# Up projections with the tokens stationary, hidden values transposed and taken by the down projection chunk by chunk, stage boundaries by token tile

## The reference

```
# model 1, layer i
f = swiglu_ffn(rmsnorm(x, ffn1_norm_pre), w_in, w_out)    # 1024 -> 2 x 2816 -> 1024
x = x + 0.5 * rmsnorm(f, ffn1_norm_post)
x = x + rmsnorm(mixer(rmsnorm(x, mix_norm_pre)), mix_norm_post)
f = swiglu_ffn(rmsnorm(x, ffn2_norm_pre), ...); x = x + 0.5 * rmsnorm(f, ffn2_norm_post)
# swiglu_ffn: (silu(gate) * up) @ w_out
# model 2, layer i (ALPHA = 8 ** 0.25)
x = layer_norm(ALPHA * x + mixer(x))
x = layer_norm(ALPHA * x + square(relu(x @ w1)) @ w2)     # 1024 -> 4096 -> 1024
x = x + sigmoid(x @ w_gate) * (p @ w_proj)
```

## Time and profile before

| | |
|---|---|
| time, median of 3 runs | 3379.53 us (3378.67 to 3382.61) |
| span of the profiled execution | 3380.1 us |
| PE busy (union of matmuls) | 3065.2 us, 91% |
| DVE busy | 2050.7 us, 61% |
| ACT busy | 1397.9 us, 41% |
| weights read | 466 MB, 138 GB/s over the span |
| mean granted TensorE clock | 0.925 of full speed |

### The profile page before, as it was taken

One profiled execution on the slowest core, in us unless ns is written; L12 is line 12 of the kernel. 1 busy time (PEld: TensorE's weight loads), 2 busy tenths in 40 slices (PEclk: granted clock), 3 DMA queues, 4 the chain that ended last, 5 costly groups with the idle time before them and its releaser, 6 DMA issues.

```text
span 3380.1 us, 48537 instructions
## 1 busy us (share of the span) xinstructions
PE 3065.2 (91%) x18678; PEld 2694.5 (80%) x18678; DVE 2050.7 (61%) x3081; ACT 1397.9 (41%) x2230; POOL 74.2 (2%) x98
## 2 busy tenths in 40 slices
PE   8999888899999998888998889976999999987998
PEld 8989766789898986677997568864897989774897
DVE  5559887555555798856555455552656665553555
ACT  4446422343433552333434334442444345442444
POOL 0000000000000000000000000000000000000000
PEclk9999999899999999988998779986999999886999
DMA  6555211255455441114553235540554555421453
GB/s 215 186 163 170 86 50 51 99 166 187 164 181 175 163 156 38 57 49 158 186 187 119 71 109 187 181 141 6 184 187 163 175 182 184 162 94 50 153 187 137
DMA packets 127386, 469.89 MB, mean 139 GB/s; under 512 B 14318, under 2 KB 14494, under 8 KB 125904
## 3 DMA queue, kind: packets, MB, share of 16 engines
q1 hardware_dynamic: 124128, 452.62, 40.0%
q0 software_dynamic: 3056, 14.39, 1.2%
HBM read 465.91 MB, written 1.05 MB: 138 GB/s over the span
## 4 chain that ended last, share of the span: by engine, by line
PE 82%; DVE 10%; ACT 4%; issue 2%; POOL 1%; DMA 0%; SPq 0%; DVEq 0%; ACTq 0%
PE ps L469 81%; DVE hc L1623 1%; DVE w_lo_part L1422 1%; ACT w_hi_part L1034 1%; PE ps L537 1%; ACT gdn_w L1248 1%; POOL stats L2044 1%; DVE x_res L1546 1%; ACT h_hi_part L1050 0%; DVE x_res L1558 0%; DVE xn L1552 0%; DVE x_res L1525 0%; DVE h_lo_part L1438 0%; DVE lke L1865 0%; DMA w_raw<-in_weights 0%
## 5 line engine op out<-in xcount | busy, mean ns | idle before, releaser
L1422 DVE TENSOR_TENSOR w_lo_part<-w_raw,w_hi_part 128x1024 fp32r<-128x1024 f32 x856 | 1028.8, 1218 | 684.7 <-ACT w_hi_part L1034 684.2
L1034 ACT ACTIVATE w_hi_part<-w_raw 128x1024 fp32r<-128x1024 f32 x856 | 884.4, 1055 | 621.2 <-PE ps L469 615.5
L469 PE MATMUL ps<-h_hi_part,w_hi_part 128*128 128x256 f32 x3424 | 987.1, 288 | 16.5 <-DVE h_lo_part L1440 11.6
L469 PE MATMUL ps<-h_lo_part,w_hi_part 128*128 128x256 f32 x3424 | 983.3, 287 | 0.0
L469 PE MATMUL ps<-h_hi_part,w_lo_part 128*128 128x256 f32 x3424 | 982.7, 287 | 0.0
L469 PEld LDWEIGHTS ps<-h_hi_part,w_hi_part 128*128 128x128 f32 x3424 | 673.3, 197 | 24.3 <-issue 17.4
L469 PEld LDWEIGHTS ps<-h_lo_part,w_hi_part 128*128 128x128 f32 x3424 | 672.9, 197 | 0.6
L469 PEld LDWEIGHTS ps<-h_hi_part,w_lo_part 128*128 128x128 f32 x3424 | 672.2, 196 | 0.0
L469 PE MATMUL ps<-w_hi_part,h_hi_part 128*128 128x512 f32 (+2 forms) x812 | 329.8, 406 | 12.3 <-DVE h_lo_part L1438 7.0
L469 PE MATMUL ps<-w_hi_part,hid_lo_part 128*128 128x512 f32 x864 | 340.9, 395 | 0.0
L469 PE MATMUL ps<-w_lo_part,hid_hi_part 128*128 128x512 f32 x864 | 340.9, 395 | 0.0
(11 more groups left out here) (307 smaller groups left out, 2590.2 us busy)
## 6 DMA issues: line engine op xcount, KB each, us to landing
w_raw<-in_weights SPq DMA_DIRECT2D x856, 512.0 KB, 3.4
row<-in_rows POOLq DMA_DIRECT2D x8, 1024.0 KB, 4.9
row<-in_rows POOLq DMA_DIRECT2D x8, 512.0 KB, 4.4
const<-in_const SPq DMA_DIRECT2D x1, 1152.0 KB, 13.8
x_res<-in_x SPq DMA_DIRECT2D x1, 1024.0 KB, 5.3
ple_p<-in_p POOLq DMA_DIRECT2D x4, 256.0 KB, 4.9
out<-x_res SPq DMA_DIRECT2D x2, 512.0 KB, 2.6
cols<-in_cols SPq DMA_DIRECT2D x1, 422.0 KB, 7.1
```

What stands on the lines that cost most here:

```text
L469: return nc.tensor.matmul(out, lhsT, rhs_, start=start, stop=stop, skip_group_check=True)
L1034: A(w_hi[:, s, 0:wd], w_raw[:, s, 0:wd], ACT.Copy).then_inc(*up("w_hi", u))
L1422: V.tensor_tensor(w_lo[:, s, 0:wd], w_raw[:, s, 0:wd], w_hi[:, s, 0:wd].bitcast(F32), ALU.subtract).then_inc(*up("w_lo", u))
```

## The change

- Up projections: a unit of a new kind "G" holds two blocks of 128 inputs by 512 outputs (256 gate and 256 up columns in a gated FFN, 512 columns in an MLP). The tokens (h_hi, h_lo, 128 x 128) are stationary and 512 weight columns move: 12 matmuls of 512 columns a unit, four units a chunk, 11 chunks in a gated FFN and 8 in an MLP. The result has the tokens on the partitions.
- The hidden values of a chunk (256 or 512 features) are transposed on PE (turn_hidden: 4 or 8 transposes) after the second unit of the next chunk, taken to hid_hi by ACT and hid_lo by DVE, and used by the down projection right behind that chunk. The last chunk's are transposed inside the first down unit of the chunk before.
- The gated FFNs no longer normalise x before the up projection: x is turned raw, with the gain applied on the way out of PSUM, and the row's root is applied in silu's scale and in the gating.
- Stage boundaries: last_units runs by tile and by half (t, n) and signals each half. Updates of x are in halves of 512. Tile 0 of x is turned at the end of the old stage, ahead of the last three matmuls for an FFN; each tile and half is taken by take_tile; the first chunk of an FFN or MLP and the first four units of a ple gate run on tile 0 first and turn tile 1 before their fourth unit. The owed splits stand one by one between these steps.
- The first transfer of x is split in two and weight unit 0 goes between.

The diff, cut to its core:

```diff
+        for c in range(FF1_N + 1):
+            if c < FF1_N:
+                hidden(a, i, c * 256, FF1 + c * 256)
+            if c:
+                for k in range(2):
+                    rows(b, i, (c - 1) * 2 + k)
...
 PE
-            def last_units(tag, parts):
+            def last_units(tag, bank, parts, nxt):
+                for t, n in ((t, n) for t in range(NT) for n in range(2)):
+                    end = t == NT - 1 and n == 1
+                    for j, (hi, lo, ready) in enumerate(parts):
...
+                        if end and j == LAST - 1 and nxt and nxt.startswith("ffn"):
+                            begin_tile(nxt, 0)
...
+                if nxt and not nxt.startswith("ffn"):
+                    begin_tile(nxt, 0)
...
+                def up_unit(s, c, j, t):
+                    tok = slice(t * P, (t + 1) * P)
+                    out = ps[:, 2 * (c % 2) + t, :]
+                    for k in (2 * j, 2 * j + 1):
+                        w = slice((k % 2) * BANK, (k % 2 + 1) * BANK)
+                        mm(out, h_hi[:, k, tok], w_hi[:, s, w], k == 0, False)
+                        mm(out, h_hi[:, k, tok], w_lo[:, s, w], False, False)
+                        last_ = mm(out, h_lo[:, k, tok], w_hi[:, s, w], False, k == KC - 1)
...
+                def turn_hidden(c):
+                    pe.wait_ge(*when("hid_gated" if blocks == 2 else "hid_square", (tag, c)))
...
+                def down_unit(c, blk):
+                    pe.wait_ge(*when("hid_lo", (tag, c, blk // 2)))
...
+                        if t == 0 and c == n - 2 and blk == 0:
+                            turn_hidden(n - 1)
...
+                tail = [(c, blk) for c in (n - 2, n - 1) for blk in range(blocks)]
+                for c, blk in tail[:-LAST]:
+                    down_unit(c, blk)
...
 ACT, ffn
+                for c in range(n):
+                    weights(2)
+                    if c:
+                        take_hidden(c - 1)
+                    weights(2)
+                    act.wait_ge(*when("w_used", ("up", tag, c)))
+                    if gated:
+                        for t in range(NT):
+                            A(act_out[:, s, t, 0:256], ps[:, 2 * s + t, 0:256], ACT.Silu, scale=st[:, 1, 4 + t:5 + t])
+                    else:
+                        A(act_out[:, s], ps[:, 2 * s:2 * s + 2, :], ACT.Relu)
+                        A(hid[:, s], act_out[:, s], ACT.Square)
+                    if 0 < c < n - 1:
+                        weights(blocks)
...
 DVE, ln into an MLP (owe(1) is one split of an owed unit)
+                link(summed(0, 0))
+                centred(0)
+                variance(0)
+                link(summed(1, 0))
+                if then.startswith("mlp"):
+                    finished(0)
+                    owe(1)
+                    centred(1)
+                    take_tile(then, 0, 0)
+                    variance(1)
+                    owe(1)
+                    take_tile(then, 0, 1)
+                    finished(1)
+                    owe(1)
+                    take_tile(then, 1, 0)
+                    take_tile(then, 1, 1)
...
 DVE, post into a mixer of model 1
+                    norm_mean(then, 0)
+                    normed(then, 0)
+                    second_half(1)
+                    owe(1)
+                    added(1)
+                    norm_mean(then, 1)
+                    normed(then, 1)
+                    owe(1)
+                    take_tile(then, 0, 0)
+                    take_tile(then, 0, 1)
+                    owe(1)
...
+                take_tile(then, 1, 0)
+                take_tile(then, 1, 1)
...
 DVE, ple into the next mixer
+                gated(1, 0)
+                if then:
+                    owe(1)
+                gated(1, 1)
+                if then:
+                    take_tile(then, 0, 0)
+                    take_tile(then, 0, 1)
+                    owe(2)
+                    take_tile(then, 1, 0)
+                    take_tile(then, 1, 1)
```

More of the change, by code:

```diff
@@ L1468, in normed, with owe, begin @@
                                 ALU.mult).then_inc(*up("xn", (tag, t)))
[L1470 removed]
+            def owe(n):
+                weights(n)
+                owed[0] -= n
+            def begin(tag, prev, key):
                 if prev == "x_in":
[L1472 to L1474 removed]
                     weights(0)
                     dve.wait_ge(sg.sem("cols_in"), 16)
[L1477 removed]
@@ L1528, in post @@
+                    for n in range(2):
+                        c = slice(n * BANK, (n + 1) * BANK)
+                        keys = [("row", r), ("end", t)] if n else []
+                        V.scalar_tensor_tensor(x[:, t, c], xn[:, t, c], st[:, 1, t:t + 1], x[:, t, c], ALU.mult,
+                                               ALU.add).then_inc(*up("x_new", (tag, t, n), *keys))
                 dve.wait_ge(*when(f"row_in{r % 2}", r))
-                scaled(0)
+                first_half(0)
@@ L2129, in unit_width @@
         return b * n * P
+    if kind == "G":
+        return UW
     k_all = K_OF.get(w, D) // P
```

662 lines of the change are left out of this document (418 added, 244 removed).

## The result

The changed kernel takes 3399.6 us (median of four runs, 3393.7 to 3406.0) where the kernel before takes 3381.1 beside it: ratio 1.005, interval 1.0037 to 1.0063. It is slower by 0.5%, some 18 us, where +7 was forecast. The profiled execution took 3393.7, the fastest of the four; its span is 3391.9, 11.8 us over that of before.

What follows compares the result with a forecast made beforehand. The prediction took TensorE (PE) matmuls to bound the kernel wherever its queue is full. Its gains and losses summed to +7.1 us on the median 3379.5, giving 3387 us, with a range of 3356 to 3406.

Steps and rivals of the forecast that it cites:

- dear up units: Up projections: rival that matmul starts lie 0.233 us apart instead of 0.227; +20 us, 3407; chance 0.12 less clock falls: 0.08.
- falls of the clock at eight ends: End of every FFN and MLP: rival that the granted clock falls behind PE's wait; 13 us, 3400; chance 0.12.
- wait at eight ends: Last chunk of every FFN and MLP: PE waits 1.85 us for hidden values behind queued splits; 14.8 us lost.
- into an FFN, three: Boundaries into three FFNs: overhead until four units are through falls from 12.2 to 4.8 us; gain 22.8 in all.
- first rival: Stage boundaries: owed splits fall into existing waits, so mixers, ples and gla.0 come out even; 3367 down to 3356; chance 0.30.
- dear bound: Up projections: matmul starts 0.233 us apart, 2.79 a unit, so the wide form gains 27 us instead of 47.4.
- Steady part: Inside FFNs and MLPs: the wider up matmuls gain 47.4 us, the transposes of hidden values cost 47.1; it comes out even.
- End of FFN and MLP: Last chunk: a split on ACT and on DVE stands ahead, PE waits 1.85 us eight times; 14.8 us lost.
- Boundaries: Between stages: gains 22.8 us into FFNs, 4.8 into MLPs; losses 7.0 and 4.9 into mixers, 4.8 ples, 3.1 gla.0.
- signs of being wrong: Prediction wrong if PE waits for splits or hid_lo in mid-FFN, or if boundaries other than the FFNs' get shorter.
- The other sign: Middle of an FFN: PE waiting for splits (w_lo) or hid_lo would show the prediction wrong; held at none.
- second rival: End of every FFN and MLP: clock falls once the wait nears 2.4 us, eight times; 13 us, 3400; chance 0.12.

Runs made afterwards that it cites:

- control: The changed kernel measured a second time without any edit: 3397.1 us, ratio to the kernel before 1.0041.
- e_double: The changed kernel with each of the 432 transposes of hidden values run twice: 3450.5 us.
- e_tail: The changed kernel with one last-chunk split each on ACT and DVE moved behind silu, relu, square and gating: 3384.5 us.
- e_order: The changed kernel with owed splits moved behind the taking of tile 1 at boundaries into mixers: 3389.4 us.
- five edits of order: The changed kernel with tail splits and owed splits moved back, tile 0 taken early, tile 1 turned before the unit's wait, start reordered: 3336.9 us.
- e_hstat: The changed kernel with blocks of h instead of hidden values stationary in the down projections, for timing alone: 3387.2 us.

## Why the prediction was right in sign and short in size

The direction was right, and 3399.6 and 3397.1 lie inside the range of 3356 to 3406. They lie above the forecast's own spread of 3374 to 3397, in a part of the range that was there for two rivals, dear up units and falls of the clock at eight ends; the first is out and the second is true for a quarter. The centre, 3387, stood only 0.7 above the bound for slower, and 19.8 us of boundary losses measured 13.7, an error that others the other way outweighed (up units 3, falls at the ends 3, mla.1 7.4). So the call of slower has some luck in it, while the mechanisms named were found where they were named. It came out at +15 (control) to +18 us and not +7. Term by term, from the two profiles of the changed kernel and those of before:

| step | forecast | measured |
|---|---|---|
| up units, 304 | -47.4 | -44 to -47 |
| 432 transposes | +47.1 | +46 (e_double's stretches) |
| wait at eight ends | +14.8 | +14.6 in waits, 12.6 back in e_tail |
| into an FFN, three | -22.8 | -21 |
| into mixers of model 1, two | +7.0 | +5.4 |
| into an MLP, four | -4.8 | -4.0 |
| into a ple, four | +4.8 | +3.3 |
| from a ple to a mixer, three | +4.9 | +3.5 |
| into gla.0 | +3.1 | +1.5 |
| start | +1.9 | about +3 |
| end | -1.5 | -1.5 |
| clock behind the eight ends | 0 | +3 (2 x 1.4) |
| inside the unchanged stages of model 2 | 0 | +6.3 (mla.1 +7.4) |
| inside the unchanged mixers of model 1 | 0 | -5.3 and -6.7 in pairs, -11.7 to -0.4 across them |

With -45 for the up units and -5.3 in the last row the measured column adds up to some +10, where the spans of that pair differ by 11.8.

The rows into an FFN, an MLP and a ple are spans until four units are through, less these units: into an FFN 23.7 - 11.5 = 12.2 before, 15.2 - 10.9 + 0.9 = 5.2 after. The other three go by the first matmul, counted from the end of the last one; the lines of rows 8 for gla.0 and from a ple start at the first transpose instead, some 0.15 us before that end.

Four of the prediction's sums don't come out of its own numbers. Into an FFN, 12.2 - 4.8 is 7.4 each and 22.2 in all, not 22.8. From a ple into a mixer, 7.2, 7.2 and 7.8 less 5.5 each make 5.7, not 4.9. The first rival's floor, 3367 less four times 2, is 3359, not 3356. And the range's upper end of 3406 is 1 us short of the dear bound that it is said to take in. Put right, the first two move the forecast from +7.1 to +8.5.

- **Steady part.** Right. The cheap price, 0.227, was the one to take, and the dear bound with its rival at 3407 is out. Over a whole FFN the mean is 0.228, which makes 3 us over the 304 units.
- **End of FFN and MLP.** Right to 0.2 us, place and cause (e_tail). By its 12.6 us this one step is most of the loss of 15 to 18, and it is an order of two calls.
- **Boundaries.** Every sign of the sum was right, the gain into the FFNs too. One of the prediction's signs of being wrong speaks against its own sum: it says that the boundaries other than the FFNs' must not get shorter, where the sum has the MLPs' 1.2 us shorter each; they came out 1.0 shorter. The other sign didn't show: PE waited for a split (w_lo) three times, 0.8 us each, at the start of an FFN and nowhere in the middle of one. Those at which a loss was forecast came out 0.4 to 1.6 us too dear each. The estimate of 1.1 for four pieces of 128 was right (1.13 on DVE into the second FFN); the queues overlapped more than written out. That is the first rival in small: "bites less" gave back 6 of its 20 us and not 20. e_order shows that the splits do bite, 14.3 us by the stretches.
- **The clock at the ends.** The second rival was priced at 13 for eight falls. Two fell, so it is true for a quarter. The prediction took the wait's length as what decides; with 1.81 to 1.86 us everywhere, it falls behind some and not behind others. By the rule of the Trainium skill that the prediction cited, doubled transposes there should have brought it down more often; they didn't.
- **What was missing** is the assumption, not written into the sum, that stretches with unchanged code keep their time. mla.1 took 7.4 us more, the largest single deviation of one stage. On balance it doesn't carry the miss, though: with the mixers of model 1, which took 5.3 and 6.7 less in the two pairs, all unchanged insides together come to +1.1 and -0.4 us. Only when the changed kernel's second profile is set against the first of before are they +6. Why the clock falls otherwise there stays open.
- **The median.** The spans of the two profiles of before are 3380.1 and 3386.0, the first near the middle of that kernel's other runs and the second near their slow end. Those of the changed kernel are 3391.9, the fastest of its four runs, and 3397.2, the slowest of control's five. Fast against fast and slow against slow they differ by 11.8 and 11.2 us, 4 to 5 more than forecast; the medians differ by 15.4 and 18.5, 8 to 11 more. So up to half of the miss lies in how the clock falls in executions of which there is no profile. A forecast from one profile can't see that.

## What to carry to other kernels

Where the matmul engine is the bound, a weight split or any other bulk work that is "ahead of need" must not stand in a strict queue in front of the short operation that the matmul engine waits for next. Write out both queues at the last chunk and at each boundary, move the bulk behind, and edit the whole boundary at once, since a wait taken away alone can reappear at the next operation of the same queue (3.25 us became 1.08 + 1.92 + 0.80). Judge such an edit by its stretches as well as by the median: 15.1 us saved at the boundaries showed as 6.7 in the time. A change that costs as much as it brings in the steady part can still be worth making for the freedom it gives the order: with five edits of order this one went from 0.5% slower to 1.3% faster. And keep some 10 us either way for granted clock in code that isn't touched: one mixer alone came out 1.7 us shorter to 10.1 longer than before.

## What the runs showed of the hardware

- The price of an fp32 matmul of 512 columns with the hidden values stationary is 0.2324 us and with h 0.227, in the same place (e_hstat); 256 columns cost 0.120 whichever operand is stationary.
- A matmul that follows a transpose starts 0.03 us later and its successor 0.31 later: going between the two is free.
- The granted clock in a stretch with waits can differ while its own work does not: the same code of mla.1 took 132.6 to 144.4 us in fourteen profiles with the same 41 us of PE idle time, and repeated to 0.1 us in the two kernels that were profiled twice. Begun at 2221.65 us in one kernel and at 2221.63 in the other it took 134.3 and 141.7, so the time since the start doesn't decide.
- The clock fell behind a PE wait of 1.81 to 1.86 us in 0 to 5 of 8 places.
